# Eight more projection panels of a two-layer decoder trunk in seven-product form

## The reference, cut to what matters

```python
def hybrid_mixer(h, w_in, sinks, conv_w, a_log, dt_bias, dn_norm_w, w_out, cos, sin):
    proj = h @ w_in
    sq, sk, sv, dn_qkv, dn_z, dn_a, dn_b = jnp.split(proj, cuts, axis=-1)
    ...
    attn_out = sliding_window_attention(sq, sk, sv, sinks)
    dn_qkv = jax.nn.silu(causal_depthwise_conv(dn_qkv, conv_w)).astype(jnp.float32)
    dq, dk, dv = jnp.split(dn_qkv, 3, axis=-1)
    ...
    o = gated_delta_rule(dq, dk, dv, g, beta)
    z = dn_z.reshape(B, S, DN_HEADS, DN_HEAD_DIM).astype(jnp.float32)
    o = (o * lax.rsqrt(jnp.mean(o * o, axis=-1, keepdims=True) + RMS_EPS)
         * dn_norm_w.astype(jnp.float32) * jax.nn.silu(z))
    ...
    return jnp.concatenate([attn_out, dn_out], axis=-1) @ w_out
```

## Time and profile before

| | us |
|---|---|
| median of 3 timed runs | 1969.96 |
| lowest, highest | 1968.98, 1971.09 |
| span of the profiled execution | 1967.6 |
| TensorE busy | 1922.2 |
| DVE busy | 701.6 |
| ACT busy | 293.9 |
| POOL busy | 107.8 |

### The profile page before, as it was taken

One profiled execution on the slowest core, in us unless ns is written; L12 is line 12 of the kernel. 1 busy time (PEld: TensorE's weight loads), 2 busy tenths in 40 slices (PEclk: granted clock), 3 DMA queues, 4 the chain that ended last, 5 costly groups with the idle time before them and its releaser, 6 DMA issues.

```text
span 1967.6 us, 27093 instructions
## 1 busy us (share of the span) xinstructions
PE 1922.2 (98%) x11373; PEld 1183.3 (60%) x11373; DVE 701.6 (36%) x1395; ACT 293.9 (15%) x595; POOL 107.8 (5%) x182
## 2 busy tenths in 40 slices
PE   8999999999999999999999999999999999999996
PEld 7888886666644444444388888866666444444442
DVE  5444335543602111011483534345535021111015
ACT  1104220110111011111111232101102111101111
POOL 3000040013000000000000000400220000000001
PEclk9999999999999999999999999999999999999999
DMA  7434342227999999999944333422189999999997
GB/s 247 150 123 134 116 160 89 65 67 292 377 404 399 421 424 412 430 427 424 394 152 150 129 129 129 138 79 86 65 346 372 410 410 421 425 414 430 428 422 277
DMA packets 124636, 539.42 MB, mean 274 GB/s; under 512 B 14704, under 2 KB 19312, under 8 KB 85360
## 3 DMA queue, kind: packets, MB, share of 16 engines
q1 hardware_dynamic: 124528, 537.86, 69.9%
HBM read 535.73 MB, written 2.10 MB: 273 GB/s over the span
## 4 chain that ended last, share of the span: by engine, by line
PE 88%; DMA 5%; DVE 5%; issue 1%; ACT 0%; SPq 0%; DVEq 0%
PE bank L1549 20%; PE bank L957 17%; PE bank L1594 10%; PE bank L968 9%; PE bank L1016 9%; PE bank L1435 6%; DMA region_b<-in_w_up_dram 4%; PE bank L1287 3%; PE bank L1050 3%; PE bank L1491 1%; PE bank L1447 1%; PE bank L1449 1%; DMA x_t<-in_w_down_dram 1%; PE bank L883 1%; PE bank L1163 1%
## 5 line engine op out<-in xcount | busy, mean ns | idle before, releaser
L957 PE MATMUL bank<-x_t,ring 128*128 128x256 f32 x1536 | 342.6, 382 | 0.0
L957 PEld LDWEIGHTS bank<-x_t,ring 128*128 128x128 f32 x1536 | 288.4, 190 | 48.8 <-issue 11.2
L2481 DVE TENSOR_TENSOR region_a<-bank,region_a 128x512 f32<-128x512 f32 x16 | 17.1, 1067 | 545.0 <-PE bank L1549 545.0
L1594 PE MATMUL bank<-ring,region_a 128*64 128x512 f32 x496 | 149.9, 602 | 0.3 <-DMA x_t<-in_w_down_dram 0.3
L1435 PEld LDWEIGHTS bank<-prob_t,x_nat 128*128 128x128 f32 x1024 | 117.9, 192 | 37.9 <-issue 37.3
L1435 PE MATMUL bank<-prob_t,x_nat 128*128 128x128 f32 x1024 | 127.1, 280 | 0.0
L968 PE MATMUL bank<-ring,mix_acc 128*128 128x512 f32 x256 | 121.3, 604 | 1.4 <-ACT mix_acc L1791 1.4
L1549 PE MATMUL bank<-ring,region_a 128*64 128x512 f32 x368 | 121.6, 595 | 0.0
L2497 DVE SCALAR_TENSOR_TENSOR y_lo<-bank,slot_gate,y_hi 128x512 fp32r<-128x512 f32 x64 | 48.0, 750 | 175.5 <-ACT y_hi L1847 171.1
L1549 PE MATMUL bank<-region_b,prob_t 128*64 128x512 f32 x368 | 97.2, 624 | 10.2 <-DMA region_b<-in_w_up_dram 10.2
L1549 PE MATMUL bank<-region_b,region_a 128*64 128x512 f32 x384 | 101.6, 597 | 0.0
(11 more groups left out here) (440 smaller groups left out, 2548.5 us busy)
## 6 DMA issues: line engine op xcount, KB each, us to landing
ring<-in_w_in_dram SPq DMA_DIRECT2D x80, 1024.0 KB, 5.0
ring<-in_w_down_dram SPq DMA_DIRECT2D x38, 1024.0 KB, 13.5
ring<-in_w_down_dram SPq DMA_DIRECT2D x18, 2048.0 KB, 13.5
ring<-in_w_gate_dram SPq DMA_DIRECT2D x34, 1024.0 KB, 9.2
ring<-in_w_out_dram SPq DMA_DIRECT2D x32, 1024.0 KB, 5.1
ring<-in_w_up_dram SPq DMA_DIRECT2D x24, 1024.0 KB, 12.9
region_b<-in_w_up_dram SPq DMA_DIRECT2D x24, 1024.0 KB, 14.4
region_b<-in_w_gate_dram SPq DMA_DIRECT2D x12, 2048.0 KB, 17.5
```

Of the source, the lines that this page charges most:

```text
L957: m = pe.matmul(b[c // 2][:, (c % 2) * T:(c % 2 + 1) * T], w[:, kk, c * P:(c + 1) * P], xT[:, k, :], start=(k == 0 and c % 2 == 0), stop=( ...
L1594: m = pe.matmul(bank[4 + c][rows, :], hid_t[:, f, rows], weights(n + e)[:, c * PANEL:(c + 1) * PANEL], start=(f == 0), stop=(f == FC - 1))
```

## The change

`FAST` grows from four panels to eleven: the convolution panels 3 to 8 and the second gate panel 10 join. Combinations of all panels from 3 on are made by POOL, which starts once DVE has made its eight. Panels 3 to 8 (`TURNED`) keep the weights, or their combination, as the stationary side: each unit is four matmuls of 128 moving columns (the tokens of one tile or their sums). All eleven use four banks each, so a panel starts when the first product of the one before is copied and goes on as the stages of its collect are done. A new `collect_turned(f)` writes the panel to `region_cd` in SBUF, and `conv(p)` reads it from there. The silu of n = 4 and 5 moves behind the ninth copy of probabilities; the copies of the first product are put between ACT's other work. Panel 10 becomes 28 filler units in place of 32, and its three collect stages stand behind levels 2, 3 and 4 of the first half's inversion. Panel 9 is now in plain order.

```diff
-    FAST = [1, 2, 9, 13]
+    FAST = [1, 2, 3, 4, 5, 6, 7, 8, 9, 10, 13]
...
-    PAIR_OF_BANKS = {0: (0, 4), 10: (0, 1), 11: (2, 3), 12: (0, 1), 14: (2, 3)}
-    PAIR_OF_BANKS.update({i: (0, 1) if i % 2 else (2, 3) for i in range(3, 9)})
-
-    FAST_BANKS = {1: (1, 2, 3, 6), 2: (0, 1, 2, 3), 9: (0, 1, 2, 3), 13: (2, 3, 0, 1)}
+    PAIR_OF_BANKS = {0: (0, 4), 11: (2, 3), 12: (0, 1), 14: (2, 3)}
+
+    FAST_BANKS = {1: (1, 2, 3, 6), 13: (2, 3, 0, 1)}
+    FAST_BANKS.update({i: (0, 1, 2, 3) for i in range(2, 11)})
...
             for l in range(depth):
+                pool.wait_ge(combined_ready.sem, combined_ready.at(l, 4 * 4 * 2))
                 for f in range(2, N_FAST):
                     for j in range(4):
                         combine(l, f, j)
...
+                        if 3 <= i <= 10 and name == "P1":
+                            pe.wait_ge(fast_copied.sem, fast_copied.at(l, f))
+                        if 3 <= i <= 10 and name in ("P2", "P5", "P4"):
+                            pe.wait_ge(fast_read.sem, fast_read.at(l, 3 * f - 2 + ("P2", "P5", "P4").index(name)))
...
                     for a in range(2):
-                        mm = pe.matmul(o, lhs[:, a, :], rhs[:, a, :], start=(j == a == 0 and name in FIRST_IN_BANK),
-                                       stop=(j == 3 and a == 1), skip_group_check=True)
-                        if name == "P1" and a == 0:
-                            settle(mm)
+                        begins, ends = j == a == 0 and name in FIRST_IN_BANK, j == 3 and a == 1
+                        if i in TURNED:
+                            for b in range(2):
+                                cols = slice(b * P, (b + 1) * P)
+                                mm = pe.matmul(o[:, cols], rhs[:, a, cols], lhs[:, a, :], start=begins and b == 0,
+                                               stop=ends, skip_group_check=True)
+                                if name == "P1" and a == b == 0:
+                                    settle(mm)
...
-                panel(3, 0, 8)
+                fast_panel(3, 0, 14)
                 turn_q(1)
-                panel(3, 8)
-
+                fast_panel(3, 14)
+
+                fast_panel(4, 0, 4)
...
-                    k_step(4, h)
-                    k_step(4, h + 1)
-                panel(5)
+                    fast_panel(4, 4 + h // 2 * 3, 7 + h // 2 * 3)
+                fast_panel(5)
...
-                panel(6, 0, 4)
+                fast_panel(6, 0, 10)
                 pe.wait_ge(probs_ready.sem, probs_ready.at(l, 1))
...
-                    for _ in range(2 if i < 3 else 1):
-                        k_step(6, owing.pop(0))
-                assert not owing
+                    fast_panel(6, 10 + 2 * i, 12 + 2 * i)
...
-                left = [(10, k, t) for k in range(KC) for t in range(NT)]
+                left = [(10, n, 0) for n in range(28)]
...
+                    if h == 11:
+                        copy_first(4)
                 act.activation(sink_e[:, :, :], sink_e[:, :, :], ACT.Exp).then_inc(exp_done.sem, 1)
-                for n in range(2, 6):
-                    silu(n)
+                silu(2)
+                silu(3)
...
+                def turned_at(f):
+                    return region_cd[:, f % 2 * 1024:f % 2 * 1024 + 5 * T]
+
+                def collect_turned(f):
+
+                    _, b, c, d = (bank[n] for n in FAST_BANKS[FAST[f]])
...
+                    tt(outer, two(b), bc(first, 1, 2), ALU.add).then_inc(fast_read.sem, 1)
+                    dve.wait_ge(fast_read.sem, fast_read.at(l, 3 * f + 1))
+                    dve.wait_ge(fast_done.sem, fast_done.at(l, 4 * f + 3))
+                    s.link(tt(inner, two(c), bc(outer[:, 1], 1, 2), ALU.add))
+                    tt(outer[:, 1], two(c)[:, 1], inner[:, 0], ALU.add).then_inc(fast_read.sem, 1)
+                    dve.wait_ge(fast_read.sem, fast_read.at(l, 3 * f + 2))
+                    dve.wait_ge(fast_done.sem, fast_done.at(l, 4 * f + 4))
                     tt(inner, two(d), inner, ALU.add).then_inc(fast_read.sem, 1)
...
                     for b in range(2):
                         n = 2 * p + b
-                        dve.wait_ge(proj_done.sem, done_at(l, i, b))
                         if n >= 2:
                             dve.wait_ge(silu_done.sem, silu_done.at(l, n - 1))
                         chunk = w * n_dn + half * HALF + 2 * b
-                        ps = bank[PAIR_OF_BANKS[i][b]]
+                        ps = turned_at(FAST.index(3 + p))[:, 2 * b * T:2 * (b + 1) * T]
...
+                collect_turned(2)
                 conv(0)
...
+                collect_turned(3)
                 dve.wait_ge(score_read.sem, score_read.at(l, n_q))
...
                 conv(1)
+                collect_turned(4)
                 dve.wait_ge(exp_done.sem, exp_done.at(l, 1))
...
+                        if half == 0 and 2 <= lev < LEVELS - 2:
+                            collect(FAST.index(10), region_cd, PANEL, q_dim, (lev - 2,))
```

141 lines of the change are left out of this document (73 added, 68 removed).

## The result

| | us |
|---|---|
| after, median of 4 runs | 2000.84 (1998.98 to 2001.79) |
| before, median of 4 runs of the same comparison | 1969.47 (1967.01 to 1971.09) |
| ratio, 95% interval | 1.0156 [1.0142, 1.017] |
| span of the profiled execution, after | 1999.4 (before 1967.6) |

The change makes the kernel 31.4 us slower, where 12.6 were forecast. The range held the time, the sign was right, the size was not. All times here are medians of fast runs; two of the twelve runs of the kernel with the gate panel alone (2018.84 and 3317.15 us) were in the slower state and are left out.

What follows compares the result with a forecast made beforehand. TensorE was taken as the bound, busy 1922 of 1967.6 us. Per layer -15.6 - 3.4 + 18.4 + 3.5 + 3.4 = +6.3, +12.6 in all: span 1980.2, time 1982.6 us, range 1944 to 2008.

Steps and rivals of the forecast that it cites:

- Part 1: Convolution panels on TensorE: 25.0 us a panel in place of 27.6, a gain of 15.6 us a layer.
- Rival D: Convolution panels: stationary loads bound the narrow matmuls, 43 us a panel, 2140 us in all; chance 0.02.
- Part 3: Convolutions: each DVE operation with two SBUF inputs costs 1.0 us more beside POOL; 19.6 us with all 12, not 7.6.
- rival C: Convolutions: the four TENSOR_SCALARs take turns with POOL too, 10 us a layer more, 2003 us; chance 0.19.
- The five delays: Scores, softmax, attention output, spread_norms(0), square_sums(1): DVE late by 3.7, 2.4, 4.6, 2.0, 5.7, sum 18.4 us a layer.
- cost at nothing: Remaining panel waits for ACT's copies and collect stages, and POOL keeping up: taken as covered, no cost.
- Part 5: Granted clock behind new mixer stalls: two drops of 1.7 us, 3.4 us a layer, between 0 and 8.
- Part 2: Second gate panel in the linear attention: 24.2 us in place of 27.6, a gain of 3.4 us a layer.
- part 4: Linear attention: POOL's combinations beside DVE's decay and mask products cost 3.5 us a layer, between 0 and 6.
- The experts' part: After the mixer: said to move with the mixer's end, since its loads start by TensorE's progress; no size given.
- A: Convolutions aren't slowed by POOL, the five places late by 1 in all: 1935 us; chance 0.12.
- B: Convolutions slowed by half as much, the five places late by 8: -7.3 us a layer, 1955 us; chance 0.25.

Runs made afterwards that it cites:

- the gate panel alone: Kernel before with only the second gate panel (panel 10) in seven-product form, its combinations by POOL, convolution panels plain: 1969.27 us, ratio 0.9999.
- POOL silent: Changed kernel with POOL's weight combinations for panels 3 to 10 one column wide instead of 512: 2053.26 us in all, convolution part of layer 1 202.76 us.
- brought back alone: Two kernels, each the reordered kernel with one move undone: the 4.4 us stall at the scores, 1957.75 us; the 6.6 us stall at square_sums(1), 1963.83 us.
- the three moves: The reordered kernel plus more panel 6 units before softmax, a collect stage inside convolution 1, a filler matmul moved to linear attention's end: 1941.23 us.
- the reordered kernel: Changed kernel with the same work in another order on TensorE, ACT and DVE, more units before waits: 1942.95 us, ratio 0.9875.
- the last one: The reordered kernel plus four small moves, with convolution 2's second silu behind the fourteenth copy of probabilities, not the ninth: 1940.37 us, ratio 0.9846.

## Why the prediction was wrong in size

**Part 1, the panels: right.** 25.0 forecast, 25.1 measured; 15.6 a layer forecast, 15.5 with POOL silent. The 0.223 us of the earlier trace rows held over 112 matmuls. Rival D is out. So is the estimate of 36.3 us a panel from the Trainium skill's 81 ns (TensorE: Matmul & The Clock Gate, section Back-to-back issue gap): a panel took 25.1.

**Part 3, POOL beside DVE: right in mechanism, by a rule that was slightly off, and in its lengths partly by luck.** The convolutions were put at 12.9 (0), 16.6 (1), 14.6 (2) and 12.9 us (5), and measured in layer 1 at 13.3, 16.7, 14.8 and 13.3. I had charged 1.0 us to each SCALAR_TENSOR_TENSOR while POOL runs. The trace says it is one charge for each instruction of POOL, whichever of DVE's it meets. The two counts agree because DVE has more instructions than POOL in such a stretch. The lengths came out near because errors cancelled: a convolution from SBUF takes 6.9 us by itself and not the 7.6 I started from, and its extra time is 6.4 to 9.8 and not 5.3 to 9.0. For convolution 0 I wrote "7 of 12 in turns", which by my own rule is 7.6 + 7.0 = 14.6, and used 12.9; it measured 13.3. The count is also why rival C's mechanism was real (the deciding row, a TENSOR_SCALAR at 1.3 us, is there: 2.46 for two at 105.32) and its price of 10 a layer was not; C's 2003 came close to the time for the wrong reason. The Trainium skill (SBUF — State Buffer, section Who interferes with whom) lists tensor_scalar among what can take the shared pair, and says that the loser blocks until the other ends; by that rule the trace agrees on both: two TENSOR_SCALARs took 2.46 us beside POOL and 0.62 with POOL silent.

**The five delays: nearly right.** Forecast and measured in layers 1 and 2: scores 3.7, 4.4 and 4.4; softmax 2.4, 0.9 and 2.5; attention output 4.6, 5.2 and 2.3; `spread_norms(0)` 2.0, 2.3 and 2.3; `square_sums(1)` 5.7, 6.6 and 6.6. Sum 18.4, 19.4 and 18.1. Left out was the wait of panel 6's P2 for the first collect stage, which I had "cost at nothing" with six units as cover: 2.3 and 1.2. conv(1) ends late by the same contention, so the cover was gone. Idle time in all is 21.6 and 19.4. This step is off by some 2 a layer.

**Part 5, the clock: the step that failed.** That the granted clock falls behind the new stalls was right; the term was too small. I took two drops a layer of 1.7 us each, 3.4, from one row of an idle time of under 2 us, and capped it at 8. Measured by the growth of busy time it is 8.5 and 12.65, the few changes of shape in it included (with POOL silent busy time is 202.54, so they are nothing to speak of). Both factors were low: there were four stretches at half clock in layer 1 and five in layer 2, not two, and they cost 2.1 and 2.5 us each in the mean, not 1.7. The longest has 5.7 us of work at 0.50, from 1281.60. The cost does not simply follow the length of the stall: the same stall of 6.6 us cost 2.2 us of clock in layer 1 and 2.8 in layer 2, and 1.5 and 2.5 where it was brought back alone; the one of 4.4 cost 1.7 in layer 1 (3.60 us at 0.53 from 119.90), and 2.9 and 3.0 where it was brought back alone. What sets the length of a stretch was not tried. The sum of the convolution part was -15.6 + 18.4 + 3.4; it is -15.6 + 20.5 + 10.6 in the mean of the layers. The 7.2 missing here, twice, are 14.4 of the 19.2 us by which the span was missed; 4.2 are the idle time.

**Part 2 and part 4, the linear attention: the sum right, the reason wrong.** I had +3.5 against -3.4 and it is -0.2 and -0.3 in all. But TensorE's work fell by 2.8, not 3.4, and I charged the 3.5 to POOL. The run with POOL silent gives it 1.0, and the one with the gate panel alone has the rest as waits of filler that ran out, 1.6 more before ACT's last copies. The text had seen that margin (5.7 at the end, 3.4 less leaves 2.3), and missed that what TensorE waits for there is not DVE's last product but ACT's copy behind the transposes.

**The experts' part: not costed.** From panel 13 to the next layer's panel 3 it takes 596.1 in place of 598.0, from the second panel 13 to the end 540.3 in place of 536.7. The kernel before has four short stretches at half clock in its experts' parts, three in the first layer and one in the second, after has one and three. At 1.7 us each that is the 3.6 of the second layer, and more than the 1.9 given back in the first. The kernel with only the gate panel changed has two and three, and 3.8 more in its last part with no stall in its convolution part; so this isn't the convolution panels' doing. It looks like scatter: from the start of the second linear attention to the end, the profiled executions of the kernels from the gate panel alone to the three moves take 694.2 to 698.9 us, with no order in them. What decides where these stretches fall was not tried.

**The rivals.** A (the convolution isn't slowed) is the run with POOL silent: 202.8 and 157.6 in place of 218.25 and 158.7 is 16.6 a layer, 1936 to 1937 by the kernel before's time, near A's 1935. B and C had the wrong multiplier, on either side.

## What to carry to other kernels

A stall of TensorE that is put in by a change costs more than its length: one of 4.4 us cost 6.9 and 7.0 here, one of 6.6 cost 8.1 and 9.1. Ask for each new wait what the clock does behind it, count every such wait, and take a range for it: the same stall gave different values in the two layers. When DVE and POOL contend, count POOL's instructions in the stretch, and then look not for a way to remove the contention but for work of TensorE to put in front of the wait: with 152 us of POOL beside 158 us of DVE in a part of 205, the reordered kernel gave back all but 2.6 of 30 us, and the last one all but 0.5. And a move that relieves one queue has to be followed through the others: copies put earlier on DVE held up a silu on ACT, and that held up TensorE.

## What the runs showed of the hardware

- A TENSOR_SCALAR of 256 columns from SBUF to SBUF takes 0.35 us alone, 0.48 from PSUM, and about 1.23 while POOL runs TENSOR_TENSORs of 512 columns. Small ones are held up too: the negation of the maxima, 32 columns, took 1.29 us (153.26 to 154.55) beside POOL and 0.17 with POOL silent.
- DVE and POOL alternate one for one: over twelve convolutions the extra time is 0.8 to 1.0 us for each of POOL's instructions of 1.27 us that run beside them. POOL itself loses little in the mean, 1.34 to 1.40 in place of 1.27. But it waits for a long instruction of DVE as DVE waits for it: at 177.00 one of POOL's took 5.38 us beside the softmax scaling, 4.42 us from 176.83.
- POOL's combinations of one column leave no trace on DVE: 0.480 and 0.350 us. It is the length of POOL's instructions that counts, not their number.
- 18 matmuls without use, put into the stall of 6.6 us in each layer, kept the granted clock at 1.00 behind it and made the kernel 5.45 us faster.
